# Attention stage with GELU built from an exponential, a spread compression chain, and groups turned and partly multiplied within the units

## What is computed

```python
# each layer, on the normed rows: one input projection, its columns shared out to four groups of 256
mla  = causal_attention(q, k, v)                    # 4 heads, 96 wide, rotary
conv = b_gate * causal_conv3(c_gate * h)
gmlp = gelu(u) * (tril(ws) @ layer_norm(gelu(v)) + bs)
kc   = gelu(blocks(kc_raw) @ w1_k) @ w2_k           # 15 compressed keys of 32 tokens
vc   = gelu(blocks(vc_raw) @ w1_v) @ w2_v           # 15 compressed values
nsa  = g0 * attend(q, kc, vc) + g1 * attend_selected(q) + g2 * attend_window(q)   # g = sigmoid(...)
x = x + concat([rms_norm(g) * gain for g in (mla, conv, gmlp, nsa)]) @ w_o
x = x + swiglu(rms_norm(x))      # layer 0 dense; layer 1: top 2 of 8 experts
```

## Time and profile before

| | us |
|---|---|
| three runs | 1464.38, 1473.96, 1462.36 |
| median | 1464.38 |
| the profiled execution, its own time | 1463.0 |
| its span in the profile | 1461.2 |
| mean granted clock of PE | 0.974 of full speed |

### The profile page before, as it was taken

One profiled execution on the slowest core, in us unless ns is written; L12 is line 12 of the kernel. 1 busy time (PEld: TensorE's weight loads), 2 busy tenths in 40 slices (PEclk: granted clock), 3 DMA queues, 4 the chain that ended last, 5 costly groups with the idle time before them and its releaser, 6 DMA issues.

```text
span 1461.2 us, 16599 instructions
## 1 busy us (share of the span) xinstructions
PE 1397.5 (96%) x6597; PEld 1014.5 (69%) x6597; DVE 819.7 (56%) x794; ACT 706.0 (48%) x773; POOL 35.6 (2%) x92
## 2 busy tenths in 40 slices
PE   8999999999899997999999999999999999999895
PEld 6875788888777756666757776757667757657574
DVE  4633544545454336646746666656546856547476
ACT  5443434343254523436535555546537546436363
POOL 2000000000000000000000000000000000000011
PEclk9979999999999897999999999999999999999998
DMA  9730756555344134999999999999999999999992
GB/s 328 241 116 1 286 177 200 173 192 177 122 149 170 62 143 187 409 409 408 403 410 409 403 385 399 409 411 409 407 398 410 410 409 402 409 410 409 403 403 111
DMA packets 148478, 444.37 MB, mean 304 GB/s; under 512 B 9454, under 2 KB 21612, under 8 KB 148396
## 3 DMA queue, kind: packets, MB, share of 16 engines
q1 hardware_dynamic: 146836, 438.24, 78.4%
q0 software_dynamic: 1440, 4.98, 0.9%
q10 hardware_dynamic: 120, 0.04, 0.0%
HBM read 439.30 MB, written 3.93 MB: 303 GB/s over the span
## 4 chain that ended last, share of the span: by engine, by line
PE 87%; DVE 5%; ACT 4%; DMA 2%; issue 1%; POOL 0%; DVEq 0%; SPq 0%; POOLq 0%; ACTq 0%
PE bank L825 84%; PE bank L828 4%; DVE ring_l L1809 1%; ACT part_h L1428 1%; DMA most<-in_moe_w_down_dram 1%; DMA ring<-in_moe_w_down_dram 1%; DVE most_l L1809 1%; DVE more_l L1809 0%; ACT prob L1622 0%; ACT xh L1428 0%; DVE y L1809 0%; DVE xT L1813 0%; ACT probT L1428 0%; ACT xn L1428 0%; DVE gm L1814 0%
## 5 line engine op out<-in xcount | busy, mean ns | idle before, releaser
L1428 ACT ACTIVATE part_h<-ring 128x2048 fp32r<-128x2048 f32 x144 | 274.0, 1917 | 135.8 <-PE bank L825 130.6
L825 PE MATMUL bank<-part_h,xh 128*128 128x512 f32 x784 | 312.4, 398 | 6.1 <-DVE xl L2220 2.5
L825 PE MATMUL bank<-part_h,xl 128*128 128x512 f32 x784 | 306.6, 391 | 0.0
L1809 DVE TENSOR_TENSOR ring_l<-ring,part_h 128x2048 fp32r<-128x2048 f32 x102 | 231.7, 2290 | 50.1 <-ACT part_h L1428 49.2
L825 PEld LDWEIGHTS bank<-part_h,xh 128*128 128x128 f32 x784 | 147.7, 188 | 46.8 <-issue 8.2
L825 PE MATMUL bank<-part_h,hTh 128*128 128x512 f32 x392 | 157.0, 401 | 17.4 <-DVE ring_l L1809 10.6
L825 PEld LDWEIGHTS bank<-part_h,xl 128*128 128x128 f32 x784 | 147.7, 188 | 31.6
L825 PE MATMUL bank<-part_h,hTl 128*128 128x512 f32 x392 | 154.8, 395 | 0.0
L1809 DVE TENSOR_TENSOR part_l<-ring,part_h 128x2048 fp32r<-128x2048 f32 x42 | 96.1, 2292 | 84.1 <-ACT part_h L1428 84.1
L1809 DVE TENSOR_TENSOR part_l<-part_in,part_h 128x2048 fp32r<-128x2048 f32 x54 | 123.1, 2290 | 32.5 <-ACT part_h L1428 32.1
L825 PE MATMUL bank<-part_l,xh 128*128 128x512 f32 x360 | 140.4, 390 | 0.0
(11 more groups left out here) (314 smaller groups left out, 1835.8 us busy)
## 6 DMA issues: line engine op xcount, KB each, us to landing
ring<-in_moe_w_down_dram SPq DMA_DIRECT2D x60, 1024.0 KB, 14.1
ring<-in_moe_w_up_dram SPq DMA_DIRECT2D x58, 1024.0 KB, 15.4
ring<-in_moe_w_gate_dram SPq DMA_DIRECT2D x50, 1024.0 KB, 13.1
part_in<-in_moe_w_down_dram SPq DMA_DIRECT2D x36, 1024.0 KB, 13.7
most<-in_moe_w_gate_dram SPq DMA_DIRECT2D x27, 1024.0 KB, 14.6
part_in<-in_moe_w_up_dram SPq DMA_DIRECT2D x27, 1024.0 KB, 13.8
part_in<-in_moe_w_gate_dram SPq DMA_DIRECT2D x21, 1024.0 KB, 16.2
most<-in_moe_w_up_dram SPq DMA_DIRECT2D x17, 1024.0 KB, 14.2
```

Source lines behind the costliest of these rows:

```text
L825: return nc.tensor.matmul(o, lhsT, rhs, start=start, stop=stop)
L1428: return nc.scalar.activation(dst, src, ACT.Copy, scale=scale)
L1809: return nc.vector.tensor_tensor(o, a, b, op)
```

## The change

ACT:

- The gate exponential moves ahead of the qT copies, together with group 1's squares; the copies to qT, kT, nqT and nkT follow.
- The chain's GELU no longer uses ACT's GELU. DVE copies the hidden values x to SBUF, makes z = x (1 + 0.044715 x²), ACT computes e = exp(-2 · 0.79788 · z), and DVE makes x / (1 + e), written to `hidT` and spread to `hidR`. The three work arrays lie in `conv_u`. The gMLP GELU stays.
- In the units: the conv_u copy goes to unit 1, group 2's squares to unit 2, e to unit 3, group 0's squares stay in unit 5, pc goes to unit 6, group 2's copy to xT to unit 7.

PE: `compress` is split in its two halves; half 0 between scores 0 and scores 1, half 1 behind values 0, hidden blocks behind values 1, compressed rows behind values 3, compressed scores behind values 4, turn_compressed and group 1's turn behind values 5, compressed values and group 2's turn behind values 6, group 0's turn behind values 7. Groups 0 to 2 all turn through bank 7. Four output products (row block 1, half 0, slices 2 to 5) run ahead of values 7 and 8; the other 28 follow in a new order.

DVE: the MLA output and the GELU arithmetic go to unit 4, the copies kcT and vcd, the scaling of groups 1 and 2 and the gate's reciprocal to unit 5, the compressed scores' masking to unit 6, group 1's copy and pcT to unit 7, group 0's scaling behind unit 8's maximum.

POOL: the group roots come in three steps, (1, 2), (0), (3).

```diff
-        TURN_BANK = (3, 2, 3, 3)
+        TURN_BANK = (7, 7, 7, 3)
+        TURN_PLACE = (2, 0, 1, 3)
...
-                compress(l)
                 scores(l, 0)
-                turn_hidden_blocks(l)
+                compress(l, 0)
                 scores(l, 1)
-                compressed_rows(l)
                 for n in range(NU):
                     turn_probs(l, n)
                     if n + 2 < NU:
                         scores(l, n + 2)
-                    if n == NU - 1:
-                        turn_group(l, 0)
+                    elif n == NU - 2:
+                        output_part(l, 1, 0, (2, 3))
+                    else:
+                        output_part(l, 1, 0, (4, 5))
                     values(l, n)
                     if n == 0:
+                        compress(l, 1)
+                    if n == 1:
+                        turn_hidden_blocks(l)
+                    if n == 3:
+                        compressed_rows(l)
+                    if n == 4:
                         compressed_scores(l)
-                    if n == 1:
+                    if n == 5:
                         turn_compressed(l)
-                    if n == 2:
+                        turn_group(l, 1)
+                    if n == 6:
                         compressed_values(l)
+                        turn_group(l, 2)
+                    if n == 7:
+                        turn_group(l, 0)
...
+            def output_part(l, b, j, ks):
+                t = 4 * (3 * l + 1)
+                q = chunk_mix[l] + NIN + 2 + j
+                ring_ready(pe, q)
+                tile = wtile[q % RING].rearrange("p (k n) -> p k n", k=KT)
+                for k in ks:
+                    g = k // 2
+                    if k % 2 == 0:
+                        pe.wait_ge(s_xTv if g % 2 else s_xTa, t + (4, 2, 2, 4)[g])
+                    i = mm(bank[WO_BANK[b][j]][:, :], xT[:, k, b * P:(b + 1) * P], tile[:, k, :],
+                           k == 2, k == KT - 1)
+                return i
...
+                output_part(l, 0, 1, (2, 3, 4, 5))
+                output_part(l, 1, 1, (2, 3, 4, 5))
+                pe.wait_ge(s_xTa, 4 * (3 * l + 1) + 4)
+                output_part(l, 0, 0, (2, 3, 4, 5, 0, 1))
+                output_part(l, 0, 1, (0, 1))
+                output_part(l, 1, 0, (0, 1))
+                output_part(l, 1, 1, (0, 1))
+                turn_group(l, 3)
...
+                act.wait_ge(s_yc, l + 1)
+                group_squares(1)
+                act.wait_ge(s_pea, NIN * (l + 1))
+                act.wait_ge(s_pev, NIN * (l + 1))
+                nc.scalar.activation(gexp[:, :, :], proj[:, :, NGL:END], ACT.Exp, scale=-1.0).then_inc(s_gex, 1)
+
                 act.wait_ge(s_qTp, l + 1)
...
-                nc.scalar.activation(hidT[:, :, 0:NC], hid_ps[:, 0, :, 0:NC], ACT.Gelu_apprx_tanh)
...
+                    if n == 1:
+                        act.wait_ge(s_hp, 2 * l + 2)
+                        copy(conv_u[:, :, :].rearrange("p b c -> p (b c)"), bank[6][:, :]).then_inc(s_hg, 1)
                     if n == 2:
...
+                        group_squares(2)
+                        squares_done(s_gms)
+                    if n == 3:
+                        act.wait_ge(s_hg, 2 * l + 2)
+                        nc.scalar.activation(hid_e, hid_z, ACT.Exp, scale=-2.0 * GELU_SCALE).then_inc(s_hr, 1)
...
+                    if n == 7:
+                        group_out(l, 2)
...
+                    if n == 3:
+                        dve.wait_ge(s_hc, l + 1)
+                        link(nc.vector.tensor_copy(hid_x, bank[6][:, 0:64]))
+                        link(tt(hid_z, hid_x, hid_x, ALU.mult))
+                        link(ts(hid_z, hid_z, GELU_CUBE, 1.0, ALU.mult, ALU.add))
+                        tt(hid_z, hid_z, hid_x, ALU.mult).then_inc(s_hg, 1)
+                    if n == 4:
...
+                        link(ts(hid_e, hid_e, 1.0, None, ALU.add))
+                        link(nc.vector.reciprocal(hid_e, hid_e))
```

More of the change, by code:

```diff
@@ L25 @@
 PI_SAFE = 3.1415925
+GELU_SCALE = 0.7978845608028654
+GELU_CUBE = 0.044715
 W = 512
@@ L191, in hybrid_trunk @@
         blk = tsb("blk", [P, 2, 2, 32, 8])
+        hid_x, hid_z, hid_e = (conv_u[:, 0, i * 64:(i + 1) * 64] for i in range(3))
         pcT = tsb("pcT", [P, NB, P])
@@ L796, in _ @@
                 root(mv[:, :, 1], rs[:, 6:6 + NB], NB, s_grs)
[L797 to L800, removed]
+                for i, (g, n) in enumerate(((1, 2 * NB), (0, NB), (3, NB))):
+                    c = 8 + NB * g
+                    pool.wait_ge(s_gms, 3 * l + i + 1)
+                    root(ms[:, c:c + n], rs[:, c:c + n], n, s_gsc)
                 for b in range(NB):
@@ L991, in turn_nsa, with compress @@
                 i.then_inc(s_nTp, 1)
[L993 to L1004, removed]
+            def compress(l, j):
+                if j == 0:
+                    pe.wait_ge(s_blk, l + 1)
+                q = chunk_mix[l] + NIN + j
+                ring_ready(pe, q)
+                w = wtile[q % RING].rearrange("p (k n) -> p k n", k=16)
+                for k in range(16):
+                    c = 32 * (k % 4)
+                    i = mm(bank[6][c:c + 32, j * CH:(j + 1) * CH], blk[:, j, k // 8, :, k % 8], w[:, k, :],
+                           k < 4, k >= 12)
+                i.then_inc(s_hp, 1)
             def turn_hidden_blocks(l):
-                pe.wait_ge(s_hg, l + 1)
+                pe.wait_ge(s_hg, 2 * l + 1)
                 for j in range(2):
@@ L2002, in row_max @@
                         negate=True).then_inc(s_mx, 1)
-                row_max(0)
-                row_max(1)
-                dve.wait_ge(s_kcp, l + 1)
-                nc.vector.tensor_copy(kcT[0:DH, 0:NC], bank[6][0:DH, 128:128 + NC])
-                for hd in range(HEADS):
-                    i = nc.vector.tensor_copy(vcd[32 * hd:32 * hd + 32, hd * DH:(hd + 1) * DH],
-                                              bank[6][32 * hd:32 * hd + 32, 192:192 + DH])
-                i.then_inc(s_kc, 1)
@@ L2039, in _ @@
                                 cvalid[:, :, None].to_broadcast([P, NB, HEADS]), ALU.mult))
[L2040 to L2056 removed]
+                    if n == 8:
+                        dve.wait_ge(s_gsc, 3 * l + 2)
+                        scale_group(0).then_inc(s_gxs, 1)
                 dve.wait_ge(s_ov, l * NU + NU)
```

127 lines of the change are left out of this document (52 added, 75 removed).

## The result

| | before | after |
|---|---|---|
| median of 20 runs each, us | 1464.41 | 1458.67 |
| lowest to highest, us | 1461.92 to 1477.21 | 1448.87 to 1465.44 |
| profiled execution, us (span) | 1463.0 (1461.2) | 1465.44 (1463.7) |
| mean granted clock of that execution | 0.974 | 0.971 |

What follows compares the result with a forecast made beforehand. PE, busy 96% of the span, was taken to bound the kernel. From the profiled 1463.0 us, 4 us of idle and 8.5 us of clock came off, giving 1450.5 us, range 1444 to 1461.

Steps and rivals of the forecast that it cites:

- signs of being wrong: Clock falling in units 1 to 3, PE waiting over 2.5 us in units 0 and 1, or scores 0 waiting for qT.
- The walk of PE: PE's order in the attention stretch: first turn 4.3 us behind the first scores, instead of 9.25 us behind 78.51.
- new waits: PE waits about 0.8 us in unit 0 and 0.5 in unit 1; ACT about 0.25 in unit 7.
- the wait of 1.32: PE's wait ahead of the first turned probabilities, 1.32 us per layer, was to vanish.
- those at the end: PE's waits in the last two units (0.84, 0.25 us) and before output products (1.1) go; the last 1.0 stays.
- GELU's small VectorE operations: Units 2 to 5: four behind maximum 3, four behind maximum 4, 1 and 1.4 us, taken as 0 for PE.
- The table load: Exponential's load ahead of the qT copies fits ACT's idle gap: 0 us, at most 0.9 us late per layer.
- The doubt: A 1.38 us drain behind each table load would overrun ACT's gap by some 1.1 us per layer; not adopted.
- Idle gain: Attention stretch: about 2.0 us less PE idle per layer, 4 us for both, bounds 0 to 6.5.
- The clock: Attention stretches at 1.2 GHz: 6.8 us still lost, between 0 and 13.6; 8.5 us back.
- case B: The forecast itself: half of the two long clock falls left, range 1446 to 1455 us; chance 0.45.
- rival E: Clock falls in unit 1 and stays low: 1461.1 us for one layer, chance 0.06; 1471.7 for both, 0.04.

Runs made afterwards that it cites:

- experiment 4: Changed kernel with the gate exponential and its table load put behind the qT and kT copies; 1451.35 us, ratio 0.9910.
- experiment 5: Only the compression chain's part of the change, groups scaled, turned and multiplied behind unit 8 as in the kernel before; 1462.29 us, ratio 0.9973.
- experiment 6: Only the groups' part of the change, compression chain and GELU as in the kernel before; 1459.82 us, ratio 0.9968.
- experiment 12: Kernel before with the groups' part of the change and 11 idle-work products of 512 columns a layer; 1443.84 us, ratio 0.9835.
- second set: The changed kernel measured once more, unedited, in 12 runs; median 1453.85 us, ratio 0.9919.
- experiment 11: Kernel before, nothing of the change, plus 11 idle-work products of 512 columns a layer; 1447.76 us, ratio 0.9874.
- experiment 10: Changed kernel with thin blocks split, table load behind qT and kT copies, 7 idle-work products of 512 columns a layer; 1460.33 us, ratio 0.9960.
- experiment 2: Changed kernel plus 13 idle-work products of 512 columns a layer in units 0, 1 and 4; 1449.37 us, ratio 0.9887.
- experiment 3: Changed kernel plus 52 idle-work products of 16 columns a layer in units 0, 1 and 4; 1487.13 us, ratio 1.0140.

## Why the prediction was right or wrong

**The outcome** fell where I put most of the chance: within 1%, 1458.67 us in a range of 1444 to 1461. But 1450.5 us was neither the profiled execution nor the median. It lies in the better group; the other one lies 10 to 15 us above. A single likeliest time hid that the clock makes two cases of this kernel. That the median fell into the range is in part luck: it depends on how many of the executions took the worse case. And by two of its own signs of being wrong the prediction was wrong: in the profiled execution the clock fell in unit 1, and scores 0 waited (for kT, which is copied together with the qT that it named).

**The walk of PE** was right: 4.42 us to the first turn (4.3 forecast); new waits of 0.79, 0.22 and 0.17 us (0.8, 0.5, 0.25); the wait of 1.32 and those at the end gone, the last, 1.1 us, left. GELU's small VectorE operations took 0.9 and 1.2 us (1 and 1.4 forecast) and nothing waited for them.

**The table load** is the step that failed among the waits. I put scores 0 at no delay because the SiLU load runs ahead of its wait, and kept "at most 0.9 us late" as a bound. It came near the bound in one layer: 0.84 and 0.43 us, which experiment 4 took away. My inference from one load to another was wrong. Why one load runs ahead of its wait and the other does not stays open: in the text of the kernel explicit waits stand ahead of both. The doubt I had drawn from the Trainium skill, ScalarE: Activation LUTs, section What ACT_TABLE_LOAD costs, was another one: its 1283 ns agree with every load seen, and its drain of 1.38 us behind them is in none of these traces (the gate exponential starts 0.01 us behind the load in experiment 4).

**Idle gain.** Forecast 2.0 us a layer; the ledger says 2.7 and 1.7 in the first trace, 1.2 and 1.5 in the second. The chain alone gave about what I forecast, -0.2 on average against 0, the kT wait included (experiment 5); the groups gave 2.9 (experiment 6) or 2.5 at full clock (experiment 12), where I had 1.95. Together that would be 2.3 to 2.7, while the mean of after's four stages is 1.8. The difference is not explained; the ledger's half weight leaves about 1 us open in one stage (76.7 and 75.5 for the chain alone). So that the mean is near the forecast is in part luck.

**The clock** is the term that was mis-sized. I took 6.8 us lost, between 0 and 13.6. Measured: 18.8 + 5.1 = 23.9 us in the slow execution, 3.4 + 1.7 = 5.1 us in the fast one. The second is my case B, and the fall stands where B put it, behind the compressed scores of unit 4. The first is rival E in one layer: fall behind the hidden products of unit 1, low through units 2 to 6 and into 7, 47.8 us low in both layers where I had allowed less than 14. I had 28 us for its length (it was 37.6: it ended only behind the first output products, in unit 7), 1461.1 us for its time (1465.44), and 0.06 for its chance, where ten of the first twenty runs stood in the group from 1461 us up (in the second set 1464.4 alone, with 1459.4 near it). What I held against it, "compress half 1, dense, lies right before", carried nothing.

**What the sum did not hold** is the price of the other way, GELU from ScalarE's own table inside the units: 1.2 us of wait in one layer, and 8 to 13 us in the median (1466.68 against 1458.67 and 1453.85). I had booked the exponential as small costs on VectorE with no return. In the runs the spread chain without it gained nothing; how the loads lead to the longer low stretches is shown for neither layer beyond the wait of 1.2 us.

**Still open.** Which of after's executions fall in unit 1 and which in unit 4 I can't say; I found nothing in the traces ahead of the fall that differs but the position in time. Nor why the wide products of experiment 11 suffice and those of experiment 10 do not: six against four stand around the compressed scores, but in experiment 2 it was six as well, and the clock fell behind them in layer 1. The scores ahead of them are of 96 rows in unit 0 and of 64 in unit 4; no run varied that alone. That the clock stays up through both stages is read from one trace each of experiments 11 and 12; all their executions lie close together, within 6.2 and 2.9 us. Open too is what before's upper group is, which no trace holds and after no longer has.

## What to carry to other kernels

Count the thin products (few columns) in a stage as a clock risk of their own, even where TensorE never idles, and read the granted clock by stretch before you reorder for idle time. Such a stage may be cheaper to fix by a few wide products, some of them in waits that are there anyway, than by spreading the thin work out; measure it, since the same remedy at other places did not always hold. And where the times of one kernel form two groups, forecast the two groups and their shares, not a mean.

## What the runs showed of the hardware that I had not expected

- The clock stayed at its lower level for 37.6 us while TensorE was busy for all 37.60 of them. The Trainium skill, TensorE: Matmul & The Clock Gate, Part 1, has the clock follow how busy TensorE has been; busy time as the profile counts it did not tell these stretches apart, wide or thin products in experiments 2 and 3 did (1449.4 and 1487.1 us).
- Instructions that do no useful work made a kernel faster by 1.3% (1463.1 to 1447.8 us in medians side by side). In the traces 11.4 of 15.2 us lie in the two stages where the clock no longer fell.
- From start to start, a one-instruction product of 16 columns took about 0.12 us (experiment 3) and one of 512 columns 0.29 (experiment 11): a thirty-second of the columns for two fifths of the time.
